# Seventeen Strassen pairs in the input projection, two filler tiles per differential head, and a reordered transition into the down projection

## The reference

```python
h = rmsnorm(x, g_mix_pre)
z = h @ w_in                         # 2048 -> 7168: 56 tiles of 128 columns
# 8 retention heads: q, k, v, gate, one tile each (32 tiles)
# 4 differential heads: q1 q2 k1 k2 v (2 tiles), 24 tiles
rq, rk = rotary(...)                 # all 128 rows of a retention q or k tile turn
dq, dk = rotary(...)                 # only the first 32 rows of a differential q or k tile turn
ret_o, state = retention_chunkwise(rq, rk, rv, s0, 128)
p = softmax(mask(q_m k_m^T * scale))   for m = 1, 2
d_o = (p_1 - lam * p_2) @ v          # prompt: causal, 4 query blocks of 128
                                     # decode: 256 past keys from 2 pages per sequence, plus the 8 new ones
x = x + rmsnorm(concat(ret_o, d_o) @ w_out)
x = x + rmsnorm(cross_attn(rmsnorm(x)))
x = x + rmsnorm(square(relu(rmsnorm(x) @ w_up)) @ w_down)   # 2048 -> 8192 -> 2048
```

## Time and profile before

| | us |
|---|---|
| median of 3 runs | 2856.57 (2854.74 to 2857.65) |
| the profiled execution's own time | 2856.25 |
| its span, first to last instruction | 2854.7 |
| PE busy | 2773.1 (97%) |
| DVE busy | 2123.6 (74%) |
| ACT busy | 1117.0 (39%) |
| POOL busy | 276.0 (10%) |

### The profile page before, as it was taken

One profiled execution on the slowest core, in us unless ns is written; L12 is line 12 of the kernel. 1 busy time (PEld: TensorE's weight loads), 2 busy tenths in 40 slices (PEclk: granted clock), 3 DMA queues, 4 the chain that ended last, 5 costly groups with the idle time before them and its releaser, 6 DMA issues.

```text
span 2854.7 us, 48366 instructions
## 1 busy us (share of the span) xinstructions
PE 2773.1 (97%) x18594; PEld 2550.3 (89%) x18594; DVE 2123.6 (74%) x2699; ACT 1117.0 (39%) x1412; POOL 276.0 (10%) x444
## 2 busy tenths in 40 slices
PE   7999998999999999998999999999989999999998
PEld 7899998988899999778899999999978888888887
DVE  5788886665666654746887777777788888888886
ACT  6343333333333333443544444444443333333332
POOL 0000001333322100000000000000010000000000
PEclk9999999999999999999999999999999999999999
DMA  6444346655667654343254444444463534544353
GB/s 217 156 122 129 109 122 183 191 188 173 196 200 237 194 182 141 92 131 91 98 160 146 142 146 143 144 145 142 135 198 121 166 106 134 154 135 148 100 181 133
DMA packets 387959, 430.37 MB, mean 151 GB/s; under 512 B 13878, under 2 KB 300844, under 8 KB 385644
## 3 DMA queue, kind: packets, MB, share of 16 engines
q1 hardware_dynamic: 346088, 269.19, 31.7%
q0 software_dynamic: 41504, 159.26, 16.3%
q10 hardware_dynamic: 228, 0.06, 0.0%
HBM read 342.21 MB, written 86.25 MB: 150 GB/s over the span
## 4 chain that ended last, share of the span: by engine, by line
PE 87%; DVE 7%; issue 2%; DMA 2%; ACT 1%; DVEq 0%; POOL 0%; ACTq 0%; SPq 0%; POOLq 0%
PE gemm L2928 22%; PE aux L3038 5%; PE aux L3040 5%; PE gemm L3038 5%; PE aux L3039 5%; PE gemm L3040 5%; PE gemm L3039 5%; PE gemm L3613 3%; PE gemm L3614 3%; PE gemm L3615 3%; PE aux L3615 3%; PE aux L3613 3%; PE aux L3614 3%; PE aux L3084 2%; PE gemm L3014 1%
## 5 line engine op out<-in xcount | busy, mean ns | idle before, releaser
L2928 PE MATMUL gemm<-act_hi,w_hi 128*128 128x288 f32 x1712 | 386.9, 308 | 17.0 <-DVE w_lo L2046 7.2
L2928 PE MATMUL gemm<-act_hi,w_lo 128*128 128x288 f32 x1712 | 369.5, 298 | 0.0
L2928 PE MATMUL gemm<-act_lo,w_hi 128*128 128x288 f32 x1712 | 369.4, 298 | 0.0
L2928 PEld LDWEIGHTS gemm<-act_hi,w_hi 128*128 128x128 f32 x1712 | 275.9, 191 | 46.5 <-issue 35.4
L2928 PEld LDWEIGHTS gemm<-act_hi,w_lo 128*128 128x128 f32 x1712 | 278.8, 191 | 0.0
L2928 PEld LDWEIGHTS gemm<-act_lo,w_hi 128*128 128x128 f32 x1712 | 278.6, 191 | 0.0
L1707 ACT ACTIVATE w_hi<-w_raw 128x2048 fp32r<-128x2048 f32 x60 | 115.2, 1919 | 306.9 <-PE aux L3615 176.0
L2574 DVE TENSOR_TENSOR w_lo<-w_raw,w_hi 128x1024 fp32r<-128x1024 f32 x120 | 146.6, 1222 | 108.3 <-ACT w_hi L1630 108.3
L1817 DVE TENSOR_TENSOR w_lo<-w_raw,w_hi 128x2048 fp32r<-128x2048 f32 x63 | 144.1, 2287 | 44.1 <-ACT w_hi L1198 43.6
L3038 PE MATMUL aux<-act_hi,w_hi 128*128 128x288 f32 x528 | 155.4, 294 | 0.0
L3040 PE MATMUL aux<-act_hi,w_lo 128*128 128x288 f32 x528 | 155.4, 294 | 0.0
(11 more groups left out here) (528 smaller groups left out, 7723.3 us busy)
## 6 DMA issues: line engine op xcount, KB each, us to landing
w_raw<-in_w_mlp_up SPq DMA_DIRECT2D x120, 512.0 KB, 4.2
w_raw<-in_w_mlp_down SPq DMA_DIRECT2D x32, 1024.0 KB, 6.3
side_hi<-in_w_mlp_down SPq DMA_DIRECT2D x32, 1024.0 KB, 7.3
w_raw<-in_w_in SPq DMA_DIRECT2D x29, 1024.0 KB, 6.5
w_raw<-in_w_in SPq DMA_DIRECT2D x54, 512.0 KB, 4.1
w_raw<-in_w_out SPq DMA_DIRECT2D x16, 1024.0 KB, 6.0
u_sum_scratch<-u_sum POOLq DMA_DIRECT2D x32, 512.0 KB, 2.9
z_scratch<-z_out SPq DMA_DIRECT2D x56, 288.0 KB, 2.4
```

Source lines behind the costliest of these rows:

```text
L2928: ins = M(out[half][:, 0:TH], w[b][:, cols], x[:, k, half * TH:(half + 1) * TH], start=first and n == 0, stop=last and n == 2)
```

## The change

Four pairs are added: v and gate of retention heads 4 to 7. Pairs with a turned tile no longer follow one another. 16 filler tiles remain, q and k of the eight retention heads; a differential head holds two (16 units), the first four retention heads two each as before. In a differential head the units stand at other places, the copies of the turned weights of rounds three and four are moved behind the last round's chain, evacuation and split of fillers are moved out of the rounds but for one split, and the key turns of the pages wait for these two copies one by one. In the transition the first down stripe is put into the buffer that is free earlier, split before the operands, and bank copies, loads, squares and sums are reordered.

```diff
-HT = 4
+HT = 2
-IN_LIST = [18, 4, 20, 6, 22, 8, (0, 2), 10, (2, 2), 12, 14, (0, 3), (2, 3)]
+IN_LIST = [18, 4, 20, 6, 22, 8, (0, 2), 10, (2, 2), 12, (0, 3), 14, (2, 3), (4, 2), (6, 2), (4, 3), (6, 3)]
-FILL = [4 * h + g for h in range(RF) for g in range(2)] + list(range(4 * RF, ZR))
+FILL = [4 * h + g for h in range(RH) for g in range(2)]
-d_fill = [4, 7, 10, 13, 16]
+d_fill = [3, 5, 7, 9, 11]
-        d11, d12, d21, d22 = w_raw[0][:], w_raw[1][:], side_flat[:, 4608:6656], side_flat[:, 6656:8704]
+        d11, d12, d21, d22 = w_raw[1][:], w_raw[0][:], side_flat[:, 4608:6656], side_flat[:, 6656:8704]
...
+            sp.wait_ge(v_add, 4 * ALL_PAIRS - 2)
+            d_load(d11, 0, 0, 0, in11)
             sp.wait_ge(v_l, 7 * ALL_PAIRS - 1)
-            d_load(d11, 0, 0, 0, in11)
             d_load(d12, 0, 0, 1, in12)
             sp.wait_ge(v_m, 7 * ALL_PAIRS - 1)
+            d_load(d21, 0, 1, 0, in21)
             d_load(d22, 0, 1, 1, in22)
-            d_load(d21, 0, 1, 0, in21)
...  POOL, transition
-            v_store(pair(UP_PAIRS - 2))
             pool.wait_ge(s_ureg, 16 * UP_PLAIN)
             for q in s_ust:
-                pool.wait_ge(q, 16 * (UP_PAIRS - 2))
-            pool.wait_ge(s_usst, 16 * (U_GROUPS - 2))
+                pool.wait_ge(q, 16 * (UP_PAIRS - 3))
+            pool.wait_ge(s_usst, 16 * (U_GROUPS - 3))
+            v_store(pair(UP_PAIRS - 2))
             pool.wait_ge(v_m, 7 * ALL_PAIRS - 4)
-            for name in ("A11", "S1", "As1", "A12", "S2"):
+            for name in ("A11", "As1", "S1", "A12"):
                 u_load(0, name)
+            s_store(pair(UP_PAIRS - 2))
             pool.wait_ge(u_h, u_count(0, "As1"))
             u_load(0, "As2")
-            s_store(pair(UP_PAIRS - 2))
-            pool.wait_ge(v_m, 7 * ALL_PAIRS - 1)
+            u_load(0, "S2")
+            pool.wait_ge(s_wlo, w_count(0, 0, 1))
...  ACT, differential heads: split(1) behind kt0 in place of split(2), none behind exp5 and sexp
...  ACT, transition
+            w_high(0, 0, 0, 0)
+            v_copy(pair(UP_PAIRS), v_e1, A[0], 7 * ALL_PAIRS - 2, 6 * ALL_PAIRS - 5)
             u_high(0, "A11")
             u_high(0, "S1")
             u_high(0, "As1")
-            v_copy(pair(UP_PAIRS), v_e1, A[0], 7 * ALL_PAIRS - 2, 6 * ALL_PAIRS - 5)
-            w_high(0, 0, 0, 0)
+            v_copy(pair(UP_PAIRS), v_u3, A[0], 7 * ALL_PAIRS, 6 * ALL_PAIRS - 2)
+            w_high(0, 0, 0, 1)
             u_high(0, "A12")
-            w_high(0, 0, 0, 1)
-            v_copy(pair(UP_PAIRS), v_u3, A[0], 7 * ALL_PAIRS, 6 * ALL_PAIRS - 2)
-            v_square(pair(UP_PAIRS), 0, 6 * ALL_PAIRS + 2)
             w_high(0, 0, 0, 2)
+            u_high(0, "S2")
+            u_high(0, "As2")
+            v_square(pair(UP_PAIRS), 0, 6 * ALL_PAIRS + 4)
             v_square(pair(UP_PAIRS), 1, 6 * ALL_PAIRS + 5)
-            u_high(0, "S2")
...  DVE, differential heads
-                    elif qb == 2:
-                        tile_take(1)
-                    elif qb == 3:
-                        split(1)
-                    after(D_PE, f"at{s}", h)
-                    dve.wait_ge(D_DVE.sem, D_DVE.before(f"at{s}", h))
-                    D_DVE.did(V.tensor_copy(d_at[:, 0:qb + 1, qb * P:(qb + 1) * P],
-                                            A[2 + qb % 2][:, 0:K].rearrange("p (c t) -> p c t", t=P)), f"at{s}")
+                    for q in ((0,), (1,), (), (2, 3))[qb]:
+                        after(D_PE, f"at{2 * q + 1}", h)
+                        dve.wait_ge(D_DVE.sem, D_DVE.before(f"at{2 * q + 1}", h))
+                        D_DVE.did(V.tensor_copy(d_at[:, 0:q + 1, q * P:(q + 1) * P],
+                                                A[2 + q % 2][:, 0:P * (q + 1)].rearrange("p (c t) -> p c t", t=P)), f"at{2 * q + 1}")
...  after the output copies
-                tile_end(2)
+                tile_end(1)
...  after the copies of the small products, around the scaling
-                tile_take(3)
                 d_scale(h, "rt", "", slice(0, TP))
-                split(3)
...  at the head's end
-                tile_end(4)
+                tile_take(2)
...  DVE, transition: w_low(0) ahead of the operands' low parts, As2 and T2 ahead of the sums, relu behind the joins
...  PE, differential heads
-                fill(0, 2)
+                fill(0, 1)
-                fill(2, 4)
+                fill(1, 3)
-                fill(16, 17)
                     for g in range(2):
+                        if p == 0:
+                            after(D_DVE, f"at{5 + 2 * g}", h)
-                after(D_DVE, "at7", h)
                 page_scores(0)
-                fill(17, 19)
                 page_keys(2)
                 page_scores(1)
-                fill(19, 21)
+                fill(11, 13)
                 page_keys(3)
                 page_scores(2)
-                fill(21, 22)
                 page_scores(3)
...
-                fill(22, 24)
+                fill(13, 15)
                 after(D_DVE, "dsel", h)
...
-                fill(24, 25)
                 after(D_DVE, "atn", h)
...
                 page_values(3)
-                fill(25, 30)
-                fill(30, 31)
                 after(D_DVE, "ot", h)
                 D_PE.did(turn(A[3][:, 0:P], d_ot[:]), "ot")
-                fill(31, 32)
+                fill(15, 16)
```

More of the change, by code:

```diff
@@ L555, in program @@
             if s % 2:
-                dn += [f"r{s - 1}", f"norm{s - 1}", f"r{s}", f"rl{s}", f"norm{s}", f"at{s}"]
+                dn += [f"r{s - 1}", f"norm{s - 1}", f"r{s}", f"rl{s}", f"norm{s}"] + [[f"at{s}"], [f"at{s}"], [], ["at5", "at7"]][s // 2]
         D_ROT = Steps(sem("d_rot"), "z t s u")
@@ L796, in _ @@
             out_load(0)
-            z_store(ZQ - 3, ZT - 3, (ZT - 3) % 2)
+            z_store(ZQ - 3, ZD + FILL[-3], 1)
             out_load(1)
@@ L803, in _ @@
                              mhi_d[RH + 2 * c:RH + 2 * c + 2].rearrange("c p t -> p c t")).then_inc(s_mixhi[c], 16)
-            z_store(ZQ - 2, ZT - 2, (ZT - 2) % 2)
+            z_store(ZQ - 2, ZD + FILL[-2], 0)
             out_load(2)
-            z_store(ZQ - 1, ZT - 1, (ZT - 1) % 2)
+            z_store(ZQ - 1, ZD + FILL[-1], 1)
             for s in range(3, 2 + RH + 1):
@@ L983, in r_load_z @@
                 for b in range(2):
-                    pool.wait_ge(s_zst[b], 16 * (ZB + (h + 1 if h < RF else 2 * h - 2)))
+                    pool.wait_ge(s_zst[b], 16 * (ZB + h + 1))
                 pool.dma_start(r_zin[h % 2][:], zr[h]).then_inc(r_zin_full[h % 2], 16)
@@ L1363, in _ @@
                         d_high(h - 1)
-                    if s == 5:
-                        split(1)
                 for p in range(DB // 2):
@@ L1374, in _ @@
                     if p == 0:
-                        split(2)
+                        split(1)
                 act.wait_ge(D_DVE.sem, D_DVE.of("o1", h))
@@ L1724, in down_pair @@
                     w_high(f, par, s, 2)
-                if s == 0:
+                if s == 0 and not skip:
                     u_high(f, "As2")
@@ L2716, in down_pair @@
                 last = isinstance(f, int) and f == FB - 1
-                t_add(f, s, "T2")
                 if not skip:
+                    t_add(f, s, "T2")
                     w_low(f, par, s, 2)
                 q_add(f, s, 1, 2)
-                if s == 0:
+                if s == 0 and not skip:
                     u_low(f, "As2")
@@ L2843, in _ @@
             tail = pair(UP_PAIRS)
+            w_low(0, 0, 0, 0)
             u_low(0, "A11")
@@ L2846, in _ @@
             u_low(0, "As1")
+            t_add(0, 0, "T1")
             v_join(tail, v_cf[0][:, TH:T], A[2], v_e1, ((v_m, tail(7, -1)), (v_e, tail(4, 1)), (v_s, tail(2, -1))))
-            w_low(0, 0, 0, 0)
-            t_add(0, 0, "T1")
-            u_low(0, "A12")
             w_low(0, 0, 0, 1)
-            v_relu(tail, 0, tail(6, 1))
             dve.wait_ge(s_usum, tail(4, 4 - 4 * IN_PAIRS))
@@ L2855, in _ @@
             v_join(tail, v_cf[1][:, 0:TH], A[3], v_u3, ())
-            v_relu(tail, 1, tail(6, 4))
+            u_low(0, "A12")
+            v_relu(tail, 0, tail(6, 1))
             w_low(0, 0, 0, 2)
             u_low(0, "S2")
+            u_low(0, "As2")
+            v_relu(tail, 1, tail(6, 4))
+            t_add(0, 0, "T2")
             dve.wait_ge(v_s, tail(2, 2))
@@ L3597, in q_product @@
                 if first and o < 3:
-                    pe.wait_ge(v_c, 6 * ALL_PAIRS + [-1, 1, 4][o])
+                    pe.wait_ge(v_c, 6 * ALL_PAIRS + [-1, 1, 3][o])
                 elif o < 2:
```

## The result

The changed kernel takes 2874.05 us (median of 6 runs, 2871.44 to 2876.70), the kernel before 2855.65 in the same session (6 runs, 2852.17 to 2857.65). The ratio is 1.0066, with a 95% interval of 1.0053 to 1.0079: slower by 0.66%. The profiled execution took 2873.97 us, with a span of 2872.4 and a mean granted clock of 0.988. The forecast was 2883, in the range 2864 to 2904, slower; the time lies in the range, just under the forecast's inner interval of 2876 to 2893.

What follows compares the result with a forecast made beforehand. PE, busy 97% of the span, was taken as the bound, with a serial DVE and ACT chain close behind in the heads. 2856.25 + 20.2 (pairs and heads) + 7.0 (retention) - 9.3 (transition) + 9 (clock) = 2883 us, range 2864 to 2904.

Steps and rivals of the forecast that it cites:

- Pairs: Strassen pair stage: four more pairs at 22.33 us each, +89.3 us, with 0 to +0.5 us a pair for stalls.
- Entry into the heads: From the pairs into differential head 0: order of loads kept, cost 0.
- Heads: Four differential heads: each 17.05 us shorter at 60.1 us, 0.9 more for head 0; -69.1 us in all before clock.
- six sections: One differential head, turn to turn, in six stretches: 23.3, 5.3, 15.3, 7.1, 3.7 and 5.4 us, 60.1 in sum.
- the ledger: Section-by-section account of a differential head: 25.9 us of filler work removed, 17.05 gained, so 8.9 us of added idle time.
- delayed copies: Softmax rounds of a differential head: moving copies behind the next round's chain helps, but the rounds remain serial; no separate size.
- Retention: Retention heads: turned evacuations delay DVE, +2.7 us at the entry, +4.1 from head 3 to 4, +0.2 in head 1; +7.0.
- Transition: Up to down projection: waits for the bank copy and As2 go, product three starts earlier; -9.3 us, bounds -4 to -11.
- product three: Down projection, counted from zero: low weights late, PE there at 2112.6, start near 2115.5 instead of 2124.84 us.
- Clock: Two half-clock spells a differential head, 9.6 us in all; 3.2 for retention and down, less 3.2 of before: +9 us.
- a spell at nearly every piece: Second rival: clock falls at nearly every idle piece of the heads, or loads land late; 2895 to 2915 us, chance 0.2.
- The first (clock stays up, 2870 to 2875): First rival, whole kernel: as forecast but the clock stays up, 2874 less 3 us; chance 0.2.

Runs made afterwards that it cites:

- Experiments 1 and 2: 1: kernel before, head 0's d_z loads issued after the stripe half, 2848.72 us; 2: pair 14 one place later in it, 2857.44; third from end in changed kernel, 2881.88.
- experiment 7: Changed kernel with the copies of turned softmax weights back in their own rounds: 2875.79 us, ratio 1.0068 to the kernel before.
- first transition kernel: Kernel before with the new transition, six filler units ahead of the last turn left out in each differential head: 2836.19 us, ratio 0.9935.
- experiment 4: Changed kernel with one filler unit of each of softmax rounds three and four moved ahead of the last turn, per differential head: 2870.37 us, ratio 1.0058.
- experiment 5: Changed kernel with the reciprocal of 512 prompt columns cut to 8 in each differential head, prompt normalisation left out: 2858.36 us, ratio 1.0009.
- experiment 6: Changed kernel with the first four retention heads' filler tiles evacuated plain, rotation of q and k of heads 4 to 7 left out: 2866.28 us, ratio 1.0039.

## Why the prediction was right, and where it was off

- *What bounds.* Right: PE in the pairs, and in the heads PE with the serial chain close behind. Sixteen units of work went per head, 25.9 us, and 8.1 us came back as waits (PE idled 2.4 us a head before and 10.5 after).
- *Pairs.* 22.27 us each against 22.33, no stall inside.
- *Entry into the heads.* This step failed: "The entry into the heads keeps its order of loads, cost 0". The program order was kept, on each engine; the order between SP and POOL was not. The waits and semaphores in the diff there are the same, but their timing hung on pair 14's place, which the diff moves. Worth 10.1 us: the wait 7.16 to 0.49, the stall 0.48, and 5.7 us of matmuls at half clock (459.18 to 464.87), 2.9. Experiments 1 and 2 show it from both sides. I had 7.16 us of PE idle in the trace before and did not ask what would become of it; it is PE's longest single wait in that trace.
- *Heads.* In head 1, five of six sections within 0.5 us; the sixth holds the spell. Over the four heads the work and waits gave 2.3 us less than the ledger said, and the clock took 2.3 less than its term: that the sum came out within 0.1 us is luck. The gain ascribed to the delayed copies is nil (experiment 7): the rounds are serial either way. That did not change the sum, since the rounds' time was taken from the chain.
- *Retention.* The two places and their sizes were right: +2.8 and +4.1, forecast 2.7 and 4.1. The clock behind these two waits, 8.0 us of work at half speed, added about 4.0 where 1.6 stood.
- *Transition.* -6.5 to down's start and -1.25 behind it, forecast -6.4 and -1.3. The first is earned; the second hides two misses. Product three came 10.7 us earlier, counted from the up projection's start (697.9 for 708.6), where 9.3 was forecast: the product that waited 3.74 us for As2 now starts without a wait, and the low weights of product three, forecast 2.8 us late, are late by 0.17 (2139.56). But behind product three the kernel now takes 732.8 us for 729.9 before, and every kernel here with the new transition takes about as long, 732.4 us or more. No spell came in the down projection, for which the forecast had 1.6 us. So -4.2 + 3.0 stands where -2.9 + 1.6 was forecast. Two new waits make 2.4 of the 3.0:

```profile
2146.29 0.50 PE L3605 MATMUL gemm<-w_hi,u_op_late 128*128 128x512 f32 x1 [1.00 <-DVE w_lo L2663]
```

```profile
2160.64 0.47 PE L3605 MATMUL gemm<-w_hi,u_op_late 128*128 128x512 f32 x1 [1.36 <-DVE y_tok L2705]
```

- *Clock.* Forecast two spells a head; there was one, at the tail wait, of 3.4 us or 6.8, and the heads lost 7.5 us to it where the forecast had 9.6. The Trainium skill ("TensorE: Matmul & The Clock Gate", section "HAM oscillation — how this bites in real kernels") tells of a clock that falls in long waits between groups of matmuls; this fits, the d_ot waits being the longest of a head. Its section "A second HAM failure mode: psum-queue depth-cycling", as the prediction read it, would have put a spell at nearly every piece; the trace of the changed kernel says no: 26 waits of 0.4 to 1.8 us in these heads, no spell at any. It does fit the kernels in which two short waits stand close together (last section).
- *Rivals.* The first (clock stays up, 2870 to 2875) holds the time measured, but for another reason: the clock did fall, in the heads by 4.1 us of matmul time more than before (15.0 us of work at half clock for 6.8), and the entry's gain covered it. So the direction and the heads' waits were foreseen; that the time lies only 9 us from the forecast owes something to errors that cancel.

## What to carry to other kernels

Filler work that hides a serial chain has its worth in that place: before it is moved to a cheaper algorithm, write down the chain of every section, and take the longer of chain and work. The same ledger wants a line for each wait that exists before, with the question whether the change moves its cause. And the order in which two queues issue competing loads is worth a wait of its own: here a 2.4 us delay of loads that were not urgent saved 6.3 us.

## What the runs showed of the hardware

- The 512 KB stripe half took 13.5 to 14.9 us to land in the four kernels where SP issued it 0.8 to 1.4 us behind the first of POOL's three d_z loads, and 3.8 to 5.2 us in the nine where it was issued 0.7 to 1.7 us ahead. How the queues share the transfers was not tested.
- Waits of PE in the differential heads and half-clock spells, over all kernels here: of 17 waits above 3 us, 17 were met by a spell. Of 10 waits between 2 and 3 us, 4 were, two of them in heads where another wait of about 1 us stood shortly ahead. Waits of 0.4 to 2 us standing alone: none, in six kernels with 18 to 32 of them each. Two waits of 0.7 to 1.2 and 1.55 us, 0.65 us apart: a spell in 21 of 28 cases (4 of 4 in three kernels, 3 of 4 in two, 2 of 4 in the kernel before, 1 of 4 in the first transition kernel). So two short waits close together did what one short wait never did; the close pairs all stand in kernels made from the one before and the lone waits in kernels made from the changed one, so other differences are not excluded. There are exceptions: ahead of or in the first retention head a wait of 3.2 us (experiment 4's kernel) and one of 3.1 us (experiment 5's) passed without a spell, and 1.67 and 1.88 us, 0.6 us apart, did so once (experiment 6's).
- The same kernel part took 77.1 or 78.7 us in two heads of one execution for such a spell alone, and the timed gains differ from the spans' by 2 to 3 us.
